# In the up product's half products, the two column pieces take turns matmul by matmul

## The chip, the cores and the metric

The kernel runs on one core of one Trainium2 chip. The metric is the device time of one launch, in microseconds. Engines are called as in the profile: PE (TensorE's matmuls), PEld (its weight loads), DVE (VectorE), ACT (ScalarE), POOL (GpSimd), SP (SyncE, which issues most transfers).

## The reference

One inference step of a one-layer trunk over 1,024 prompt tokens and 32 sample tokens: an attention mixer, then a feed-forward part with a short convolution. The part that the change touches is the first product of the feed-forward part:

```
def conv_ffn(h, conv_past, w_up, conv_w, conv_b, w_down):
    u, g = jnp.split(jnp.einsum('btd,df->btf', h, w_up), 2, axis=-1)
    u_ext = jnp.concatenate([conv_past.astype(u.dtype), u], axis=1)
    c = conv_b + u_ext[:, 0:t] * conv_w[0]
    ...
    y = jax.nn.gelu(c, approximate=True) * g
    return jnp.einsum('btf,fd->btd', y, w_down), u_ext[:, -(CONV_W - 1):]
```

All values are fp32. `h` is 1,056 x 1,024 (prompt and sample tokens together), `w_up` is 1,024 x 5,632, and `D_FF` is 2,816.

## The kernel before

**Precision.** Every fp32 operand is held as a high and a low part in a replicated fp32 type (`m_h`, `m_l` for the tokens, `ring_h`, `ring_l` or `ws_h`, `ws_l` for weights). Each product is three matmuls: high weights by high tokens, high weights by low tokens, low weights by high tokens. The helper `three` (lines 1095, 1096, 1097) issues them on one output bank. Each of these matmuls has a weight load of its own in the trace, also where two in a row use the same weights.

**The up product.** It runs over f = 0 to 21, one step for each 128 columns of u and of v. The first three steps (`plain_products`) are ordinary: 8 pieces of 24 matmuls, each piece on one bank. The other 19 (`split_products`, f = 3 to 21) use a scheme of seven half-size products in place of eight, P1, P6, P2, P7, P5, P4, P3 in this order. A half product multiplies a 512-row by 128-column weight block with 528 tokens. The 528 tokens are two column pieces of `CB` = 264, c = 0 and c = 1, each with its own PSUM bank. A piece is 4 row blocks by 3 matmuls, 12 matmuls of 264 columns. So one f is 7 x 2 x 12 = 168 matmuls and the 19 split steps hold 3,192.

**Banks.** P1 and P2 use banks 0 and 1, P6, P7 and P4 banks 2 and 3, P5 and P3 banks 4 and 5. P1, P6 and P5 start a bank afresh; P2, P7, P4 and P3 add onto what the earlier product left there. In between, the partial result has to be read out: after P1 by ACT into `p1s` (`p1_out`, line 1617 is the copy helper), after P6 and P7 by DVE into `u2s` and `u3s` (`u_sum`, line 2838), after P5, P4 and P3 by DVE into `uv` and `uext` (`out_sum`, line 2850), after P2 by ACT into `uext` (`c11_out`). Each product on a bank waits until the read before it is done. Between a product and the next that uses its banks there lies at least one whole other product.

**What else runs.** POOL forms the sums of weight blocks and the low parts (`weight_sums`, `weight_lows`), ACT the high parts (`weight_high`), each after the product that last used the slot has finished its piece 1. DVE also does the convolution (`conv_taps`, lines 2775 to 2784) and the gate (`gated`, line 2792) of f - 1, in one queue with the sums: taps 0 and 1, `u2` twice, tap 2, `u3` twice, `c22` twice, the gate, `c21` twice, `c12` twice. At f = 3 it has token preparation to do as well (`token_low`). All engines take their instructions in the written order. After f = 21 the down product begins (`step_tile`, matmuls of 512 columns, lines 1101 to 1103).

**Order inside a half product.** Piece 0 runs all of its 12 matmuls, then piece 1 all of its own:

```
for c in range(2):
    pe.wait_ge(up_act, act_evicted(f, "p1", c))
    half_product(f, "P2", c, c, m_h[:, 4:8, 0:HB], m_l[:, 4:8, 0:HB], False)
```

Of the kernel before, what the change touches and what calls it, by code (L numbers as in the profile page):

```python
# [16 lines left out]
TOK = SEQ + DEC  # L17
# [51 lines left out]
HB = TOK // 2  # L69
CB = HB // 2  # L70
# [55 lines left out]
def program(nc, x_prompt, x_sample, cache_fox_k, cache_fox_v, cache_fox_logf, cache_swa_k, cache_swa_v,  # L126
# [17 lines left out]
    def place(name, shape, dt=F32, offset=None):  # L144

        size = 4 * int(np.prod(shape[1:]))
        o = at[0] if offset is None else offset
        if offset is None:
            at[0] += (size + 31) // 32 * 32
        return nc.alloc_sbuf_tensor_at(name, shape, dt, offset=o), o  # L150
# [91 lines left out]
    m_h, _ = place("m_h", [P, KT, TOK], F32R, offset=R3)  # L242
    m_l, _ = place("m_l", [P, KT, TOK], F32R, offset=R3 + 4 * KT * TOK)
# [18 lines left out]
    tb = []  # L262
# [89 lines left out]
    bank = [nc.alloc_psum_tensor(f"bank{i}", [P, 512], F32) for i in range(8)]  # L352
# [71 lines left out]
    up_full = sem("up_full")  # L424
    up_act = sem("up_act")
    up_dve = sem("up_dve")
# [76 lines left out]
    def plain_evicted(f, kind_, t, c):  # L503
        return len(PLAIN_ORDER) * f + PLAIN_ORDER.index((kind_, t, c)) + 1

    def act_evicted(f, what, c):

        return len(PLAIN_ORDER) * PLAIN + 4 * (f - PLAIN) + dict(p1=0, c11=2)[what] + c + 1

    def dve_evicted(f, what, c):  # L510

        return 10 * (f - PLAIN) + 2 * ["u2", "u3", "c22", "c21", "c12"].index(what) + c + 1

    def blocks_made(f, name):

        return 7 * (f - PLAIN) + PRODUCTS.index(name) + 1
# [179 lines left out]
    def mix_bank(t, e):  # L696

        return bank[((7, 0), (1, 2), (3, 4))[t % 3][e]]

    def sbank(i):  # L700
        return bank[3 + i % 2]

    def merge_bank(i):

        return bank[(7, 0, 1, 2, 3, 4)[i % 6]]
# [53 lines left out]
    with nc.Block() as block:  # L759

        def flat(slot):
            return slot.rearrange("p k c -> p (k c)")
# [165 lines left out]
        def slot(name):  # L928

            i = dict(P1=0, P2=1, P6=2, P4=3, P7=4, P5=5, P3=6)[name]  # L930
            if i == 6:
                return ws_h[:, :, :], ws_l[:, :, :]
            return tuple(w[:, i // 2, 4 * (i % 2):4 * (i % 2) + 4, :] for w in (ring_h, ring_l))
# [158 lines left out]
        def _(pe):  # L1092
            def three(out, wh, wl, xh, xl, start, stop, onto=False):

                nc.tensor.matmul(out, wh, xh, start=start, stop=False, skip_group_check=onto)  # L1095
                nc.tensor.matmul(out, wh, xl, start=False, stop=False, skip_group_check=onto)  # L1096
                return nc.tensor.matmul(out, wl, xh, start=False, stop=stop, skip_group_check=onto)  # L1097

            def three_moving(out, th, tl, wh, wl, start, stop, onto=False):

                nc.tensor.matmul(out, th, wh, start=start, stop=False, skip_group_check=onto)  # L1101
                nc.tensor.matmul(out, th, wl, start=False, stop=False, skip_group_check=onto)  # L1102
                return nc.tensor.matmul(out, tl, wh, start=False, stop=stop, skip_group_check=onto)  # L1103
# [70 lines left out]
            for k in range(4):  # L1174
                mm = nc.tensor.transpose(bank[3][0:HEADS, P * k:P * k + P], cln[:, k, :], ident)
            mm.then_inc(misc_pe, 1)
            for k in range(6):
                mm = nc.tensor.transpose(bank[4][:, FT * k:FT * k + FT], cvn[:, k, :], ident[0:FT, 0:FT])
# [108 lines left out]
            for g in range(2):  # L1287
                for i, (o, w) in enumerate(((0, PAST), (PAST, DEC))):
                    s = S_SMP + 2 * g + i
                    pe.wait_ge(s_free, s - 1)  # L1290
                    for e in range(2):
                        mm = nc.tensor.matmul(sbank(s)[:, 0:w], qbd[:, 2 * g + e, :], ktc[:, 2 * g + e, o:o + w],
                                              start=(e == 0), stop=(e == 1))
# [4 lines left out]
            for g in range(2):  # L1298
# [7 lines left out]
                for e in range(2):  # L1306
                    pr = 2 * g + e
                    for k in range(5):
                        v = past[:, k, P * pr:P * pr + P] if k < 4 else fresh[0:DEC, P * pr:P * pr + P]
                        r = DEC if k == 4 else P  # L1310
                        mm = nc.tensor.matmul(bank[7][:, P * pr:P * pr + P], v, pts[0:r, k, :],
                                              start=(k == 0), stop=(k == 4))
# [88 lines left out]
            for i in range(3 * KT):  # L1401
                s, e, c = i // 6, i // 3 % 2, i % 3
                n = SLAB["ws", s]
                wh, wl = (flat(w[:, n % NSPL]).rearrange("p (k c) -> p k c", k=4)[:, :, P * e:P * e + P]
                          for w in (ring_h, ring_l))
# [7 lines left out]
                for k in range(4):  # L1413
                    mm = three(merge_bank(i)[:, 0:CH], wh[:, k, :], wl[:, k, :], ot_h[:, k, CH * c:CH * c + CH],
                               ot_l[:, k, CH * c:CH * c + CH], k == 0, k == 3)
# [10 lines left out]
            for t in range(NT + 1):  # L1426
# [4 lines left out]
                for e in range(2):  # L1431
# [3 lines left out]
                    for k in range(KT):  # L1435
# [3 lines left out]
                        elif t == 0 and (e == 0 or last):  # L1439
                            pe.wait_ge(slab_split, SLAB["wo", k] + 1)  # L1440
                        wh = wo_last_h[:, cols_e] if last else wo[k][:, 0, cols_e]
                        wl = wo_last_l[e][:, :] if last else wo[k][:, 1, cols_e]
                        mm = three_moving(mix_bank(t, e)[0:r, :], m_h[:, k, P * t:P * t + r],
                                          m_l[:, k, P * t:P * t + r], wh, wl, k == 0, last)
# [25 lines left out]
                                   k == 0, k == KT - 1)  # L1470
                    mm.then_inc(up_full, 1)

            def half_product(f, name, c, b, xh, xl, fresh_bank):

                pe.wait_ge(w_ready, blocks_made(f, name))
                wh, wl = slot(name)
                for k in range(4):
                    mm = three(bank[b][:, 0:CB], wh[:, k, :], wl[:, k, :], xh[:, k, CB * c:CB * c + CB],
                               xl[:, k, CB * c:CB * c + CB], fresh_bank and k == 0, k == 3, not fresh_bank)
                mm.then_inc(up_full, 1)  # L1480

            def split_products(f):

                first = f == PLAIN
                for c in range(2):
                    pe.wait_ge(up_act, plain_evicted(f - 1, "u", 0, c) if first else act_evicted(f - 1, "c11", c))
                    half_product(f, "P1", c, c, m_h[:, 0:4, 0:HB], m_l[:, 0:4, 0:HB], True)
                if first:
                    pe.wait_ge(t_ready[2], 1)
                for c in range(2):  # L1490
                    if first:
                        pe.wait_ge(up_act, plain_evicted(f - 1, "v", 0, c))
                    else:
                        pe.wait_ge(up_dve, dve_evicted(f - 1, "c21", c))
                    half_product(f, "P6", c, 2 + c, tb[0][0], tb[0][1], True)
                for c in range(2):
                    pe.wait_ge(up_act, act_evicted(f, "p1", c))
                    half_product(f, "P2", c, c, m_h[:, 4:8, 0:HB], m_l[:, 4:8, 0:HB], False)
                if first:
                    pe.wait_ge(t_ready[3], 1)  # L1500
                for c in range(2):
                    pe.wait_ge(up_dve, dve_evicted(f, "u2", c))
                    half_product(f, "P7", c, 2 + c, tb[1][0], tb[1][1], False)
                if first:
                    pe.wait_ge(t_ready[1], 1)
                for c in range(2):
                    if first:
                        pe.wait_ge(up_act, plain_evicted(f - 1, "u", 1, c))
                    else:
                        pe.wait_ge(up_dve, dve_evicted(f - 1, "c12", c))  # L1510
                    half_product(f, "P5", c, 4 + c, m_h[:, 0:4, HB:TOK], m_l[:, 0:4, HB:TOK], True)
                if first:
                    pe.wait_ge(t_ready[0], 1)
                for c in range(2):
                    pe.wait_ge(up_dve, dve_evicted(f, "u3", c))
                    half_product(f, "P4", c, 2 + c, tb[2][0], tb[2][1], False)
                for c in range(2):
                    pe.wait_ge(up_dve, dve_evicted(f, "c22", c))
                    half_product(f, "P3", c, 4 + c, m_h[:, 4:8, HB:TOK], m_l[:, 4:8, HB:TOK], False)

            for f in range(PLAIN):
                plain_products(f)
            for f in range(PLAIN, FT):
                split_products(f)
# [24 lines left out]
            def step_tile(name, k, t):  # L1549

                if k == 0:
                    wait_out_bank(name, t)
                ah, al, bh, bl = ops[step(name, k) % NOP]
                fresh = name in FRESH
                c = slice(P * t, P * t + P)
                return three_moving(bank[PRODUCT_BANKS[name][t]][:, :], ah[:, c], al[:, c], bh[:, :], bl[:, :],
                                    fresh and k == 0, k == HK - 1, not fresh)
# [27 lines left out]
            for name in DOWN:  # L1585
                last = name == DOWN[-1]
                for k in range(HK - GROUP if last else HK):
                    wait_operands(step(name, k))
                    if name == "P2" and k == 0:
                        pe.wait_ge(conv_done, FT)  # L1590
                        pe.wait_ge(up_dve, dve_evicted(FT - 1, "c12", 1))
                        for w in range(4):
                            mm = nc.tensor.transpose(bank[5][0:FT, P * w:P * w + P], tails[:, w, :], ident)
                        mm.then_inc(misc_pe, 1)
                    for t in range(4):
                        if t == 3 and name in SAMPLE:
                            step_sample(name, k)
                        mm = step_tile(name, k, t)
# [3 lines left out]
            for k in range(HK - GROUP, HK):  # L1602
                wait_operands(step("P3", k))
                mm = step_sample("P3", k)
            mm.then_inc(sample_full, 1)
            for t in range(4):
                for k in range(HK - GROUP, HK):
                    mm = step_tile("P3", k, t)
# [1449 lines left out]
```

## Time and profile before

| | |
|---|---|
| median of 3 runs | 1567.58 us (1566.83 to 1568.66) |
| the profiled execution's own time | 1569.79 us |
| its span, first to last instruction | 1568.0 us |
| outside the span | 1.79 us |
| PE busy | 1506.5 us, 96% |
| PEld busy | 1405.5 us, 90% |
| DVE / ACT / POOL busy | 1028.7 / 599.9 / 617.4 us |
| mean granted TensorE clock | 0.989 of full speed |

The profiled execution took 2.21 us longer than the median of the runs. Matmuls overlap each other in the trace: each is drawn 0.28 us long, but starts about 0.12 us after the one before. So the distance from start to start, called the pitch below, is what a matmul costs, not its drawn length. The timeline gives starts to 0.01 us.

### The profile page before, as it was taken

To read this page: it belongs to the slowest core of one execution; us is meant where nothing else is said; L and a number is where in the kernel's file an instruction comes from. 1 tells how busy PE (TensorE), PEld (TensorE's weight loads), DVE (VectorE), ACT (ScalarE), POOL (GpSimd) and SP (SyncE) were. 2 spreads that over 40 slices of the span, in tenths; PEclk is the share of its full clock that TensorE was granted. 3 is DMA by queue.
4 is the path that set the end of the run, shared out by engine and by line. 5 is a ranking of instruction groups with operands and counts; after the bars stand their busy time and mean duration, and the time that the engine had idled before them with its cause. 6 is when DMAs were issued, how large, how long until landed. Compare 5 with 4: busy or idle time off the path is not lost.

```text
span 1568.0 us, 25757 instructions
## 1 busy us (share of the span) xinstructions
PE 1506.5 (96%) x9819; PEld 1405.5 (90%) x9819; DVE 1028.7 (66%) x2020; ACT 599.9 (38%) x1248; POOL 617.4 (39%) x405
## 2 busy tenths in 40 slices
PE   6999999999999999999999999999999999999996
PEld 5899999999998988889787999999999999778885
DVE  6866667767674359866444796655555555578976
ACT  5133534435341235646323243233333322444463
POOL 6522232222221332225231568878787782000104
PEclk9999999999999999999999999999999999999998
DMA  6232222222122630128431112322222228723557
GB/s 197 69 87 69 73 91 65 73 69 69 30 96 74 233 105 27 52 67 287 163 114 58 44 56 83 95 73 79 80 70 70 82 83 275 243 92 114 177 189 136
DMA packets 156185, 164.87 MB, mean 105 GB/s; under 512 B 13973, under 2 KB 121881, under 8 KB 156065
## 3 DMA queue, kind: packets, MB, share of 16 engines
q1 hardware_dynamic: 119113, 108.30, 21.9%
q10 hardware_dynamic: 34840, 51.14, 9.7%
q0 software_dynamic: 2112, 3.80, 1.7%
q8 instruction: 79, 1.29, 0.3%
q14 instruction: 41, 0.34, 0.1%
HBM read 125.03 MB, written 39.85 MB: 105 GB/s over the span
## 4 chain that ended last, share of the span: by engine, by line
PE 78%; DVE 13%; ACT 2%; DMA 2%; issue 2%; POOL 2%; ACTq 1%; SPq 0%; DVEq 0%; POOLq 0%
PE bank L1095 16%; PE bank L1097 15%; PE bank L1096 15%; PE bank L1101 6%; PE bank L1103 6%; PE bank L1102 6%; PE bank L1127 4%; PE bank L1236 2%; PE bank L1207 1%; PE bank L1206 1%; DVE rowsn L2335 1%; DVE kl L2356 1%; DMA fox<-d_mfox 1%; PE bank L1575 1%; PE bank L1577 1%
## 5 line engine op out<-in xcount | busy, mean ns | idle before, releaser
L943 POOL TENSOR_TENSOR ring_h<-raw,att 128x1024 fp32r<-128x1024 f32 x48 | 101.7, 2119 | 511.4 <-PE bank L1097 501.8
L1095 PE MATMUL bank<-ht_h,ring_h 128*128 128x352 f32 x816 | 270.3, 331 | 2.0 <-POOL ring_l L944 1.6
L1097 PE MATMUL bank<-ht_h,ring_l 128*128 128x352 f32 x816 | 264.7, 324 | 0.0
L1096 PE MATMUL bank<-ht_l,ring_h 128*128 128x352 f32 x816 | 264.0, 324 | 0.0
L1095 PE MATMUL bank<-m_h,ring_h 128*128 128x264 f32 x648 | 184.2, 284 | 2.6 <-POOL ring_l L1035 1.3
L1096 PE MATMUL bank<-m_l,ring_h 128*128 128x264 f32 x648 | 184.2, 284 | 0.0
L1097 PE MATMUL bank<-m_h,ring_l 128*128 128x264 f32 x648 | 183.9, 284 | 0.0
L1095 PEld LDWEIGHTS bank<-ht_h,ring_h 128*128 128x128 f32 x816 | 155.0, 190 | 5.5 <-POOL ring_l L944 2.1
L1096 PEld LDWEIGHTS bank<-ht_l,ring_h 128*128 128x128 f32 x816 | 155.7, 191 | 0.7
L1097 PEld LDWEIGHTS bank<-ht_h,ring_l 128*128 128x128 f32 x816 | 155.1, 190 | 0.0
L944 POOL TENSOR_TENSOR ring_l<-raw,ring_h 128x1024 fp32r<-128x1024 f32 x48 | 129.8, 2704 | 3.8
L1095 PE MATMUL bank<-tb_h,ring_h 128*128 128x264 f32 x456 | 129.9, 285 | 0.0
L1097 PE MATMUL bank<-tb_h,ring_l 128*128 128x264 f32 x456 | 129.6, 284 | 0.0
L1096 PE MATMUL bank<-tb_l,ring_h 128*128 128x264 f32 x456 | 129.6, 284 | 0.0
L1095 PEld LDWEIGHTS bank<-m_h,ring_h 128*128 128x128 f32 x648 | 121.9, 188 | 3.0 <-ACT uext L1617 1.5
L1097 PEld LDWEIGHTS bank<-m_h,ring_l 128*128 128x128 f32 x648 | 122.0, 188 | 0.0
L1096 PEld LDWEIGHTS bank<-m_l,ring_h 128*128 128x128 f32 x648 | 121.7, 188 | 0.0
L1103 PE MATMUL bank<-op_bh,op_al 128*128 128x512 f32 x308 | 120.3, 391 | 0.0
L1102 PE MATMUL bank<-op_bl,op_ah 128*128 128x512 f32 x308 | 120.2, 390 | 0.0
L1101 PE MATMUL bank<-op_bh,op_ah 128*128 128x512 f32 x308 | 120.0, 389 | 0.0
L2412 DVE CUSTOM_DVE_ANT_0 ssb<-bank,negc 128x512 f32<-128x512 f32 (+2 forms) x96 | 50.9, 555 | 73.4 <-PE bank L1210 44.5
L1035 POOL TENSOR_TENSOR ring_l<-sw,ring_h 128x512 fp32r<-128x512 f32 x57 | 91.4, 1606 | 4.7 <-ACT ring_h L1617 4.7
(367 smaller groups left out, 3839.1 us busy)
## 6 DMA issues: line engine op xcount, KB each, us to landing
raw<-in_w_up SPq DMA_DIRECT2D x44, 512.0 KB, 3.8
raw<-in_w_in SPq DMA_DIRECT2D x34, 512.0 KB, 3.8
rb<-in_w_down SPq DMA_DIRECT2D x66, 256.0 KB, 2.9
d_y<-conv SPq DMA_DIRECT2D x22, 529.0 KB, 3.0
d_gate<-gst ACTq DMA_DIRECT2D x48, 176.0 KB, 1.9
a<-d_y SPq DMA_DIRECT2D x33, 256.0 KB, 5.5
ra<-d_y SPq DMA_DIRECT2D x33, 256.0 KB, 3.2
gm<-d_gate ACTq DMA_DIRECT2D x8, 528.0 KB, 4.2
```

The costliest lines, as they stand in the source:

```text
L943: order.link(nc.gpsimd.tensor_tensor(high, src, zero.to_broadcast(list(src.shape)), ALU.add))
L944: nc.gpsimd.tensor_tensor(low, src, high.bitcast(F32), ALU.subtract).then_inc(slab_split, 1)
L1035: nc.gpsimd.tensor_tensor(l, x, h.bitcast(F32), ALU.subtract).then_inc(w_ready, 1)
L1095: nc.tensor.matmul(out, wh, xh, start=start, stop=False, skip_group_check=onto)
L1096: nc.tensor.matmul(out, wh, xl, start=False, stop=False, skip_group_check=onto)
L1097: return nc.tensor.matmul(out, wl, xh, start=False, stop=stop, skip_group_check=onto)
L1101: nc.tensor.matmul(out, th, wh, start=start, stop=False, skip_group_check=onto)
L1102: nc.tensor.matmul(out, th, wl, start=False, stop=False, skip_group_check=onto)
L1103: return nc.tensor.matmul(out, tl, wh, start=False, stop=stop, skip_group_check=onto)
L1127: last = nc.tensor.transpose(o, i, ident[0:i.shape[0], 0:i.shape[0]])
L1236: nc.tensor.matmul(bank[7][:, o:SPAN], vhl[:, k, h, :], pt[:, k, o:SPAN], start=False, stop=False)
L2412: V.tensor_tensor_reduce(out=ssb[:, s % 2, o:o + w], in0=sbank(sc)[:, 0:w], in1=negc[:, h, o:o + w], scale=1.0, scalar=-3e38, op0=ALU.add, ...
```

## The change

The helper `half_product`, which did one piece, becomes `both_halves`, which does both: for every row block and each of the three terms it issues the matmul of piece 0 on bank b and then that of piece 1 on bank b + 1, with the same weights. The number of matmuls, their shapes, operands and banks, and the order of sums within each bank stay. The waits of both pieces now stand ahead of the first matmul of the product, and both pieces finish on its last two matmuls.

```
-            def half_product(f, name, c, b, xh, xl, fresh_bank):
+            def both_halves(f, name, b, xh, xl, fresh_bank):
                 pe.wait_ge(w_ready, blocks_made(f, name))
                 wh, wl = slot(name)
                 for k in range(4):
-                    mm = three(bank[b][:, 0:CB], wh[:, k, :], wl[:, k, :], xh[:, k, CB * c:CB * c + CB],
-                               xl[:, k, CB * c:CB * c + CB], fresh_bank and k == 0, k == 3, not fresh_bank)
-                mm.then_inc(up_full, 1)
+                    for i, (w, x) in enumerate(((wh, xh), (wh, xl), (wl, xh))):
+                        for c in range(2):
+                            mm = nc.tensor.matmul(bank[b + c][:, 0:CB], w[:, k, :], x[:, k, CB * c:CB * c + CB],
+                                                  start=fresh_bank and k == 0 and i == 0, stop=k == 3 and i == 2,
+                                                  skip_group_check=not fresh_bank)
+                            if k == 3 and i == 2:
+                                mm.then_inc(up_full, 1)
...
                 for c in range(2):
                     pe.wait_ge(up_act, plain_evicted(f - 1, "u", 0, c) if first else act_evicted(f - 1, "c11", c))
-                    half_product(f, "P1", c, c, m_h[:, 0:4, 0:HB], m_l[:, 0:4, 0:HB], True)
+                both_halves(f, "P1", 0, m_h[:, 0:4, 0:HB], m_l[:, 0:4, 0:HB], True)
...
-                for c in range(2):
-                    pe.wait_ge(up_act, act_evicted(f, "p1", c))
-                    half_product(f, "P2", c, c, m_h[:, 4:8, 0:HB], m_l[:, 4:8, 0:HB], False)
+                pe.wait_ge(up_act, act_evicted(f, "p1", 1))
+                both_halves(f, "P2", 0, m_h[:, 4:8, 0:HB], m_l[:, 4:8, 0:HB], False)
...
-                for c in range(2):
-                    pe.wait_ge(up_dve, dve_evicted(f, "u2", c))
-                    half_product(f, "P7", c, 2 + c, tb[1][0], tb[1][1], False)
+                pe.wait_ge(up_dve, dve_evicted(f, "u2", 1))
+                both_halves(f, "P7", 2, tb[1][0], tb[1][1], False)
```

P6, P5, P4 and P3 are changed in the same way: P6 and P5 keep the waits of both pieces, now ahead of both, and P4 and P3 wait for `u3` and `c22` of piece 1.

## Rows read from the trace of the kernel before

**Rows 1.** The page: its head, and busy time of PE, PEld and DVE.

```profile
span 1568.0 us, 25757 instructions
PE 1506.5 (96%) x9819; PEld 1405.5 (90%) x9819; DVE 1028.7 (66%) x2020; ACT 599.9 (38%) x1248; POOL 617.4 (39%) x405
```

**Rows 2.** Windows: the split stage, then the plain stage (busy us, count, clock).

```profile
965.00:1322.00 357.00, 357.00 (x2939) 357.00 (x2939) 202.80 (x336) 111.81 (x210) 274.97 (x187) 1.00 0.29 92
877.00:931.00 54.00, 54.00 (x446) 54.00 (x446) 52.13 (x26) 15.36 (x27) 32.44 (x10) 1.00 0.13 40
```

**Rows 3.** The chain that ended last, from 965 to 1322 us, by line.

```profile
by line: PE bank L1097 33.4%; PE bank L1096 33.3%; PE bank L1095 33.3%
```

**Rows 4.** Timeline of PE: ends of pieces in one round (start, drawn us, instruction).

```profile
1099.26 0.28 PE L1097 MATMUL bank<-m_h,ring_l 128*128 128x264 f32 x1
1099.38 0.28 PE L1095 MATMUL bank<-m_h,ring_h 128*128 128x264 f32 x1
...
1103.64 0.28 PE L1097 MATMUL bank<-tb_h,ring_l 128*128 128x264 f32 x1
...
1106.67 0.28 PE L1095 MATMUL bank<-tb_h,ring_h 128*128 128x264 f32 x1
```

**Rows 5.** Timeline of PE: last matmuls of pieces, plain stage, then split stage.

```profile
884.45 0.28 PE L1097 MATMUL bank<-m_h,ring_l 128*128 128x264 f32 x1
...
931.13 0.28 PE L1097 MATMUL bank<-m_h,ring_l 128*128 128x264 f32 x1
932.75 0.36 PE L1095 MATMUL bank<-m_h,ring_h 128*128 128x264 f32 x1 [1.34 <-POOL ring_l L1035]
...
965.07 0.28 PE L1097 MATMUL bank<-tb_h,ring_l 128*128 128x264 f32 x1
...
1116.76 0.28 PE L1097 MATMUL bank<-m_h,ws_l 128*128 128x264 f32 x1
...
1118.20 0.28 PE L1097 MATMUL bank<-m_h,ws_l 128*128 128x264 f32 x1
...
1119.68 0.28 PE L1097 MATMUL bank<-m_h,ring_l 128*128 128x264 f32 x1
...
1322.40 0.28 PE L1097 MATMUL bank<-m_h,ws_l 128*128 128x264 f32 x1
```

**Rows 6.** Timeline of DVE: piece 1 of two sums, then both pieces of one.

```profile
1103.96 0.43 DVE L2838 TENSOR_TENSOR u2s<-bank,p1s 128x264 f32<-128x264 f32 x1 [0.97 <-PE bank L1097]
...
1118.52 0.50 DVE L2850 TENSOR_TENSOR uext<-bank,u2s 128x232 f32<-128x232 f32 x2 [1.01 <-PE bank L1097]
...
939.01 0.77 DVE L2838 TENSOR_TENSOR u2s<-bank,p1s 128x264 f32<-128x264 f32 x2
```

**Rows 7.** Timeline of ACT: both pieces of one copy out of PSUM.

```profile
1108.62 0.65 ACT L1617 ACTIVATE uext<-bank 128x264 f32<-128x264 f32 x2
```

**Rows 8.** Timelines of DVE, then of PE, in the second split step (f = 4).

```profile
956.54 0.76 DVE L2850 TENSOR_TENSOR uv<-bank,p1s 128x264 f32<-128x264 f32 x2
...
963.13 0.77 DVE L2838 TENSOR_TENSOR u2s<-bank,p1s 128x264 f32<-128x264 f32 x2
...
963.39 0.28 PE L1097 MATMUL bank<-m_h,ring_l 128*128 128x264 f32 x1
963.62 0.39 PE L1095 MATMUL bank<-tb_h,ring_h 128*128 128x264 f32 x1
```

**Rows 9.** A window at the lower clock; timelines of PE there and later.

```profile
81.00:87.00 6.00, 6.00 (x24) 0.50 0.54 123
...
82.47 0.49 PE L1097 MATMUL bank<-ht_h,ring_l 128*128 128x352 f32 x1
82.76 0.49 PE L1095 MATMUL bank<-ht_h,ring_h 128*128 128x352 f32 x1
...
630.22 0.32 PE L1097 MATMUL bank<-ht_h,ring_l 128*128 128x352 f32 x1
630.38 0.32 PE L1095 MATMUL bank<-ht_h,ring_h 128*128 128x352 f32 x1
```

More of the change, by code:

```diff
@@ L1494, in split_products @@
                         pe.wait_ge(up_dve, dve_evicted(f - 1, "c21", c))
-                    half_product(f, "P6", c, 2 + c, tb[0][0], tb[0][1], True)
-                for c in range(2):
-                    pe.wait_ge(up_act, act_evicted(f, "p1", c))
-                    half_product(f, "P2", c, c, m_h[:, 4:8, 0:HB], m_l[:, 4:8, 0:HB], False)
+                both_halves(f, "P6", 2, tb[0][0], tb[0][1], True)
+                pe.wait_ge(up_act, act_evicted(f, "p1", 1))
+                both_halves(f, "P2", 0, m_h[:, 4:8, 0:HB], m_l[:, 4:8, 0:HB], False)
                 if first:
                     pe.wait_ge(t_ready[3], 1)
-                for c in range(2):
-                    pe.wait_ge(up_dve, dve_evicted(f, "u2", c))
-                    half_product(f, "P7", c, 2 + c, tb[1][0], tb[1][1], False)
+                pe.wait_ge(up_dve, dve_evicted(f, "u2", 1))
+                both_halves(f, "P7", 2, tb[1][0], tb[1][1], False)
                 if first:
@@ L1510, in split_products @@
                         pe.wait_ge(up_dve, dve_evicted(f - 1, "c12", c))
-                    half_product(f, "P5", c, 4 + c, m_h[:, 0:4, HB:TOK], m_l[:, 0:4, HB:TOK], True)
+                both_halves(f, "P5", 4, m_h[:, 0:4, HB:TOK], m_l[:, 0:4, HB:TOK], True)
                 if first:
                     pe.wait_ge(t_ready[0], 1)
[L1514 to L1519, printed above, removed]
+                pe.wait_ge(up_dve, dve_evicted(f, "u3", 1))
+                both_halves(f, "P4", 2, tb[2][0], tb[2][1], False)
+                pe.wait_ge(up_dve, dve_evicted(f, "c22", 1))
+                both_halves(f, "P3", 4, m_h[:, 4:8, HB:TOK], m_l[:, 4:8, HB:TOK], False)
             for f in range(PLAIN):
```

## The prediction

> **What bounds the kernel now.** I read the page first. PE is busy for 96% of the span, DVE for 66% [rows 1], so the question is whether the change makes PE's stream shorter or puts holes into it. The windows come next. From 965 to 1322 us, where 17 of the 19 split steps and most of another run, PE is busy in all 357 us and the granted clock is 1.00, the 2.4 GHz level [rows 2]. The chain of waits over the same stretch holds nothing but the three lines of the matmul helper, a third each [rows 3]: PE waits for nobody there. What sets the stage is the pitch times the number of matmuls.
>
> The pitch comes from counted matmuls between two starts. From 965.07 us (the last matmul of piece 0 of P7 at f = 4) to 1322.40 us (the last one of f = 21) there are 7 pieces of f = 4 and 17 steps of 168, so 84 + 2,856 = 2,940 matmuls in 357.33 us: 121.54 ns each [rows 5]. All 3,192 of the split steps at that pitch are 388.0 us, 25% of the time. One nanosecond of pitch is worth 3.19 us, which is 0.20% of the time, and 0.2% (3.1 us) is about what a measurement of this kernel can tell from no change.
>
> **The change, part by part.**
>
> *The same matmuls in another order.* Nothing is added or removed: 3,192 matmuls with 3,192 loads stay. What moves is the bank: before, PE goes to another bank after 12 matmuls, after the change it does so at every one. A run of one matmul per bank is not in the trace, so I bound its cost by how the pitch reacts to changes of bank that are there.
>
> First the single step. Piece 0 of P1 ends at 1099.26 us and piece 1 begins in the other bank at 1099.38, a pitch of 0.12 us [rows 4], like that within a piece. If writing onto the same bank again were what costs the pitch its excess, the matmul behind a change of bank would start earlier, and it does not, to the 0.01 us that the view gives.
>
> Then the mean. In the plain stage a bank takes 24 matmuls in a row, in the split stage 12. From 884.45 to 931.13 us lie the 16 pieces of 24 of f = 1 and 2, 384 matmuls in 46.68 us, 121.56 ns each [rows 5]. Twice as many changes of bank per matmul leave the pitch where it was, 121.54 against 121.56. The rounding of the starts makes that 0.02 +- 0.03 ns in favour of more changes. The step from 24 to 12 adds one change per 24 matmuls, the change under study adds 22 per 24 more. Stretched by 22, the difference is -0.5 +- 0.7 ns, so -1.5 us with ends at -3.6 and +0.6 us. I do not take that mean as the value, because the two stages read other tiles and the reading order matters too.
>
> How much it matters is seen in the pieces. Twelve matmuls of the last piece of P3 take 1.44 us (1116.76 to 1118.20), the twelve of the next P1 take 1.48 us (1118.20 to 1119.68) [rows 5], 120 against 123 ns, with the same shapes and no wait. So an order of operand addresses can be worth a nanosecond or two in a single piece. Over all fourteen pieces of a step these differences average out at 121.5. After the change the addresses stay and only their order is new. I take 0 as the value. For the ends I take half of the difference between these pieces and the mean, 0.75 ns below and above, so -2.4 and +2.4 us. The lower end by the stretched difference, -3.6 us, reaches further and takes its place.
>
> *Same weights twice as often.* Before, one matmul in three has the weights of the matmul before it (the first two of a triple); after, four in six. Each keeps its own load; now there is one for every matmul [rows 1]. In a triple the starts are 0.12 us apart whether the weights are new or not, so I cost this at nothing, within the ends above.
>
> *The waits of both pieces come first.* In a steady step this is hidden. P6 ends with a matmul at 1103.64 us, DVE begins the sum of piece 1 at 1103.96, 0.32 us later, and is done 0.43 us after that [rows 4, 6]. After the change both pieces are full at that same moment. Two sums in a row take 0.77 us [rows 6], so the second is read at 0.32 + 0.77 = 1.09 us behind the last matmul's start. P7, which needs both, begins at 1106.67 us, 3.03 us behind it [rows 4]. The cover left is 1.9 us. It is P2, a whole product of 24 x 121.5 = 2.92 us. The same holds for P7 to P4, P5 to P3 and P4 to the next P6, each with one or more products between. The read of piece 1 after P3 comes in two instructions, together 0.50 us in place of 0.43 [rows 6], which makes the pair 0.77 + 0.07 = 0.84 us, still far below. ACT's copies of both pieces take 0.65 us [rows 7].
>
> What queues behind the later reads: on DVE, taps 0 and 1 of the convolution follow the two `c12` sums. Before, piece 0 was read during piece 1's matmuls; now both wait for the end, so the taps start 0.34 us later (0.84 - 0.50). DVE idled 0.97 us before the last `u2` sum and 1.01 us before the last `c12` sum [rows 6], so it catches up before the next product needs it. On ACT the weight copies behind `p1_out` start 0.3 us later. They feed weights of the step after, a step of 20.4 us away, and POOL's work is released by the piece 1 that ends when it did. No transfer is issued by an engine that becomes later by more than this.
>
> *Start of the split stage.* DVE is behind there, since it prepares tokens. At f = 4 it begins the two `u2` sums at 963.13 us and is done at 963.90 [rows 8]. P7's first matmul starts at 963.62 us, 0.23 us behind the one before in place of 0.12, since it waits for the first sum only (963.13 + 0.43 = 963.56, and 0.06 us for the signal). After the change it waits for both: 963.90 + 0.06 = 963.96 us. That is +0.34 us, once. The `c21` sums of f = 3 are both done by 956.54 + 0.76 = 957.30 us [rows 8], before P6 of f = 4 needs them: P2 ends at 963.39 + 0.12 = 963.51, two products less is 957.67. That cover is 0.37 us. At f = 5 and later nothing of this is left, as the chain shows [rows 3]. The last step hands over to the down product with DVE's queue 0.3 us later, which lies behind a whole down step that does not need it.
>
> *The sum.* Pitch 0, steady waits 0, start +0.34 us, end 0: the profiled execution's 1569.79 us becomes 1570.13. It stood 2.21 us above the median of the runs, so the median to expect is 1567.9 us.
>
> **The rivals.**
>
> *Coming back to the same bank is what costs (faster).* At 2.4 GHz and a column per cycle 264 columns are 110.0 ns; the pitch is 121.5 [rows 2, 5]. Matmuls of 352 columns follow each other at 160 ns (630.22 to 630.38) [rows 9], 38.5 ns for 88 more columns, 0.44 ns each, so about 115 of the 121.5 goes with the columns. If the rest, 6 to 11.5 ns, were a wait for the last write to the same bank, alternating would save 19 to 37 us and give 1531 to 1549 us. Against it stands the step between banks at 0.12 us. A weaker form, 1 to 3 ns, is what the pieces' differences allow: 1558 to 1564.5 us. The Trainium skill (TensorE: Matmul & The Clock Gate, "Back-to-back issue gap") gives a bare gap of 112.5 ns for this width, and says that in a stream of loads and matmuls both set the spacing; by the bare gap the sum would be 28.8 us lower, but it names no cost of a bank, and the trace shows 121.5.
>
> *The new order is a bad one (slower).* Each matmul reads 1,056 bytes further on in the same row and then back; if the pieces' slow pattern (123 ns) became the rule, 1.5 ns x 3,192 = 4.8 us, 1567.9 + 4.8 = 1572.7 us. It decides from 1 ns on.
>
> *The reads are no longer covered (slower).* If a product had to wait for the second read in every step, as at f = 4, it would cost 0.34 us x 19 = 6.5 us for each such product, 1574 us. It decides when DVE reaches the pair 1.9 us or more late. The idle time of 1 us ahead of its sums speaks against it.
>
> *The clock falls (slower).* A stretch at granted clock 0.50, the 1.2 GHz level, is in the trace from 81 to 87 us; matmuls of 352 columns follow each other there at 0.29 us against 0.16 [rows 9]. Six such microseconds cost 6 x (1 - 0.16 / 0.29) = 2.7 us. In the split stage it is 1.00 throughout, and the one new hole is 0.34 us, shorter than the 1.62 us from 931.13 to 932.75 us that are there now, between the two windows at 1.00 [rows 2, 5]. The Trainium skill (TensorE: Matmul & The Clock Gate, "A second HAM failure mode: psum-queue depth-cycling") speaks against such a change: a kernel that cycled through banks idled briefly and often, and its clock went up and down. Here the pairs leave no gap for that, and this rival gets 1 in 100.
>
> **How the numbers follow.** The forecast, a time within 0.2% of before: 0.72. Faster through the bank: 0.14. Slower through the order: 0.10, through uncovered reads: 0.03, through the clock: 0.01. So faster 0.14, same 0.72, slower 0.14. The likeliest case alone spans 1567.9 - 3.6 = 1564.3 to 1567.9 + 2.4 = 1570.3. The range is drawn a little wider to take in the near parts of the two pitch rivals: 1564.0 to 1571.2 us.
>
> **What the profile after would show.** The pitch over the counted 2,940 matmuls between 121 and 122 ns, the clock at 1.00, the chain in that stretch still only matmul lines, DVE's `u2` sums as pairs of 0.77 us begun 0.3 us behind P6, and P7 at f = 4 starting 0.34 us later. The prediction is wrong if the pitch moves by more than 1 ns, which the view of starts shows at once, or if the view of waits names DVE or ACT ahead of a product after f = 4.

## The result and the profile after

The changed kernel takes 1570.76 us (median of 12 runs, 1567.8 to 1575.71) against 1567.53 us (12 runs, 1564.53 to 1570.48) for the kernel before. The ratio is 1.0023, with a 95% interval from 1.0013 to 1.0032: 3.2 us slower (2.0 to 5.0 us by the interval), a small loss, but the interval lies above 1. The time is inside the range of the prediction, 0.4 us below its upper end, but the likeliest case there (a time within 0.2% of before) put its upper end at 1570.3 us. The rival "the new order is a bad one", at 1572.7 us, is nearer than the forecast of 1567.9 us.

The page of the changed kernel says almost nothing. Its span is 0.4 us longer than that before [rows 1]:

```profile
span 1568.4 us, 25626 instructions
PE 1505.3 (96%) x9819; PEld 1405.0 (90%) x9819; DVE 1031.9 (66%) x2020; ACT 598.1 (38%) x1248; POOL 619.5 (39%) x405
```

The window of the split stage in the changed kernel shows more. Its columns are those of [rows 2]:

```profile
930.30:1323.30 393.00, 391.58 (x3191) 391.18 (x3192) 231.31 (x362) 122.15 (x235) 305.70 (x204) 1.00 0.29 92
```

The stage began 2.4 us earlier here than in [rows 5], by differences in stages that the change does not touch, and this hides most of the loss in the span of this one execution. So the stage has to be compared alone. PE's timeline after the change gives the first matmul of the split stage, the first of f = 5, and the first of the down product:

```profile
930.37 0.48 PE L1480 MATMUL bank<-m_h,ring_h 128*128 128x264 f32 x2 [1.34 <-POOL ring_l L1035]
...
973.35 0.41 PE L1480 MATMUL bank<-m_h,ring_h 128*128 128x264 f32 x2
...
1323.43 0.39 PE L1101 MATMUL bank<-op_bh,op_ah 128*128 128x512 f32 x1
```

The stage takes 1323.43 - 930.37 = 393.06 us. Before it took 389.77 us, from 932.75 to 1322.52, one pitch behind the last row of [rows 5]. That is +3.29 us, and the medians differ by 3.23 us. The 17 steps from f = 5 on hold 2,856 matmuls in 350.08 us: 20.593 us for a step and 122.58 ns for a matmul. In the kernel before, the same two starts are

```profile
975.38 0.28 PE L1095 MATMUL bank<-m_h,ring_h 128*128 128x264 f32 x1
...
1322.52 0.39 PE L1101 MATMUL bank<-op_bh,op_ah 128*128 128x512 f32 x1
```

so 347.14 us, 20.420 us for a step and 121.55 ns for a matmul. The pitch has grown by 1.03 ns.

Nothing waits there. The chain of the changed kernel from 965 to 1322 us is the one matmul line, as in [rows 3]:

```profile
by line: PE bank L1480 100.0%
964.98 357.03 PE bank L1480 x2913
```

The reads of the banks went as forecast. DVE's timeline in one step after the change, then PE's around it (P6's last matmuls and P7's first):

```profile
1102.95 0.77 DVE L2838 TENSOR_TENSOR u2s<-bank,p1s 128x264 f32<-128x264 f32 x2 [1.92 <-PE bank L1480]
```

```profile
1102.57 0.41 PE L1480 MATMUL bank<-tb_h,ring_l 128*128 128x264 f32 x2
1102.81 0.41 PE L1480 MATMUL bank<-m_h,ring_h 128*128 128x264 f32 x2
...
1105.76 0.40 PE L1480 MATMUL bank<-tb_h,ring_h 128*128 128x264 f32 x2
```

The last matmul of P6 is the second of the pair at 1102.57, so at about 1102.69. The pair of sums begins 0.26 us behind it, lasts 0.77 us and ends at 1103.72, 2.04 us before P7 begins. DVE had been idle for 1.92 us before it. At f = 4 the new wait shows:

```profile
960.73 0.77 DVE L2838 TENSOR_TENSOR u2s<-bank,p1s 128x264 f32<-128x264 f32 x2
```

```profile
960.97 0.41 PE L1480 MATMUL bank<-m_h,ring_l 128*128 128x264 f32 x2
961.55 0.51 PE L1480 MATMUL bank<-tb_h,ring_h 128*128 128x264 f32 x2 [0.17 <-DVE u2s L2838]
```

P7 starts at 961.55, 0.05 us after the pair of sums ends at 961.50. Its distance from the matmul before (961.10) is 0.45 us; it was 0.23 us in [rows 8].

### The profile page after: what moved, and what is told of

It reads as the page before. It is cut to its first block, busy times and chain, and to the rows that moved or that the text cites. A ratio compares the mean times of both kernels' runs of the same rounds, so it can differ in the third digit from the quotient of the medians.

```text
span 1568.4 us, 25626 instructions
## 1 busy us (share of the span) xinstructions
PE 1505.3 (96%) x9819; PEld 1405.0 (90%) x9819; DVE 1031.9 (66%) x2020; ACT 598.1 (38%) x1248; POOL 619.5 (39%) x405
## 4 chain that ended last, share of the span: by engine, by line
PE 76%; DVE 13%; POOL 3%; DMA 2%; ACT 2%; issue 2%; ACTq 1%; SPq 0%; DVEq 0%; POOLq 0%
PE bank L1480 23%; PE bank L1095 8%; PE bank L1097 7%; PE bank L1096 7%; PE bank L1101 6%; PE bank L1103 6%; PE bank L1102 6%; PE bank L1127 4%; PE bank L1236 2%; PE bank L1207 1%; PE bank L1206 1%; DVE rowsn L2335 1%; DMA fox<-d_mfox 1%; POOL ring_l L1035 1%; DVE kl L2356 1%
## 5 line engine op out<-in xcount | busy, mean ns | idle before, releaser
L1035 POOL TENSOR_TENSOR ring_l<-sw,ring_h 128x512 fp32r<-128x512 f32 x57 | 94.6, 1664 | 4.8 <-ACT ring_h L1617 4.7
L1480 PE MATMUL bank<-m_h,ring_h 128*128 128x264 f32 x456 | 92.9, 285 | 2.5 <-POOL ring_l L1035 1.3
L1480 PE MATMUL bank<-m_h,ring_l 128*128 128x264 f32 x456 | 93.5, 287 | 0.0
L1480 PE MATMUL bank<-tb_h,ring_l 128*128 128x264 f32 x456 | 93.2, 286 | 0.0
L1480 PE MATMUL bank<-tb_h,ring_h 128*128 128x264 f32 x456 | 92.8, 285 | 0.2 <-DVE u2s L2838 0.2
L1480 PE MATMUL bank<-m_l,ring_h 128*128 128x264 f32 x456 | 92.9, 285 | 0.0
L1480 PE MATMUL bank<-tb_l,ring_h 128*128 128x264 f32 x456 | 92.7, 285 | 0.0
L1617 ACT ACTIVATE pt_h<-bank 128x512 fp32r<-128x512 f32 (+2 forms) x96 | 43.6, 488 | 122.9 <-PE bank L1237 86.3
L1617 ACT ACTIVATE ring_h<-sw 128x512 fp32r<-128x512 f32 x57 | 35.6, 632 | 142.7 <-POOL sw L1028 122.9
L1786 ACT ACTIVATE ssb<-ssb,att 128x128 f32<-128x128 f32 (+3 forms) x64 | 49.7, 777 | 82.7 <-DVE att L2419 82.6
```

The lines of the kernel that those rows point to most:

```text
L1035: nc.gpsimd.tensor_tensor(l, x, h.bitcast(F32), ALU.subtract).then_inc(w_ready, 1)
L1480: mm = nc.tensor.matmul(bank[b + c][:, 0:CB], w[:, k, :], x[:, k, CB * c:CB * c + CB], start=fresh_bank and k == 0 and i == 0, stop=k == 3 ...
L1617: return nc.scalar.activation(out, in_, cp, scale=scale)
```

## The experiments

The question was which part of the change costs a nanosecond per matmul. All kernels are made from the changed one. They replace the loops of `both_halves` by this body, in which weights, tokens and banks each have a sequence of their own. In the cuts below, what stands behind a `#` is a note for the reader.

```
+                after = [(k, i, c) for k in range(4) for i in range(3) for c in range(2)]
+                before = [(k, i, c) for c in range(2) for k in range(4) for i in range(3)]
+                weights, moving, banks = ...
+                place_of = [c for _, _, c in banks]
+                for j in range(24):
+                    (kw, iw, _), (kx, ix, cx), c = weights[j], moving[j], place_of[j]
...
+                    mm = nc.tensor.matmul(bank[b + c][:, 0:CB], terms[iw][0][:, kw, :],
+                                          terms[ix][1][:, kx, CB * cx:CB * cx + CB], ...)
```

The figure to compare is the steady step: the start of f = 5 to the start of the down product, divided by 17. Within a trace the 17 steps agree to 1 ns, with one exception of 12 ns in all traces, and kernels that read the tokens in the same order have the same step in traces taken on different chips, so one profile of each is enough to tell 0.01 us. The distance between P2's last matmul and P7's first at f = 4 is given as "the hole".

**Only the waits.**

```
+                weights, moving, banks = before, before, before
```

> The waits of both pieces stand ahead of the product, as in the changed kernel, but piece 0 then runs its 12 matmuls and piece 1 its own, as before. The loss of the change is 0.17 us in each steady round of 168 matmuls (20.59 against 20.42 us) and about 0.3 us once at f = 4. Theory A, the order of matmuls is what costs: the steady round is 20.42 us here, the step at f = 4 stays late by about 0.3 us, in all 0.3 us over the kernel before. Theory B, the waits in front cost something in every round: the round is 20.59 us here too, and the time is 3 us over the kernel before.

```profile
974.91 0.28 PE L1485 MATMUL bank<-m_h,ring_h 128*128 128x264 f32 x1
...
1322.05 0.39 PE L1101 MATMUL bank<-op_bh,op_ah 128*128 128x512 f32 x1
```

347.14 / 17 = 20.420 us, the step of the kernel before. The hole is 0.51 us; it was 0.23 us before and is 0.45 us in the changed kernel. The time is 1567.98 us (10 runs) against 1566.92 (13 runs), a ratio of 1.0 (0.9989 to 1.0011), which rules out the 3 us of theory B as well. Theory A holds: the waits in front cost a few tenths once, the order of the matmuls costs the rest.

**Only the banks, and only the reads.**

```
+                weights, moving, banks = before, before, after    # banks only
+                weights, moving, banks = after, after, before     # reads only
```

> The 24 matmuls of a product read weights and tokens in the order of the kernel before, and write the banks b, b + 1, b, b + 1 in turn. What is summed in a bank is thus not the product of its own piece; the amount of work, the waits and all shapes stay. Theory A1, the change of bank at each matmul costs 1 ns: the steady round is 20.59 us. Theory A2, the order in which operands are read costs: the round is 20.42 us.

> The counterpart: weights and tokens are read in the order of the changed kernel, and the first 12 matmuls write bank b, the next 12 bank b + 1. What is summed in a bank is not the product of its own piece; the amount of work, the waits and all shapes stay. Theory A1, change of bank: the steady round is 20.42 us. Theory A2, order of the reads: 20.59 us. If both share in it, the two runs add up to 20.59 - 20.42 = 0.17 us over the round before.

PE's timeline with the banks in turn:

```profile
970.50 0.28 PE L1485 MATMUL bank<-m_h,ring_h 128*128 128x264 f32 x1
...
1317.64 0.39 PE L1101 MATMUL bank<-op_bh,op_ah 128*128 128x512 f32 x1
```

and with the reads in the new order:

```profile
971.55 0.41 PE L1485 MATMUL bank<-m_h,ring_h 128*128 128x264 f32 x2
...
1321.63 0.39 PE L1101 MATMUL bank<-op_bh,op_ah 128*128 128x512 f32 x1
```

Banks in turn: 347.14 / 17 = 20.420 us. Reads in the new order: 350.08 / 17 = 20.593 us. In this stream a change of bank at every matmul costs nothing and gains nothing; the whole loss of the steady step follows the order in which operands are read.

**Triples in turn.** Three matmuls of piece 0, three of piece 1, on their own banks:

```
+                triple = [(k, i, c) for k in range(4) for c in range(2) for i in range(3)]
+                weights, moving, banks = triple, triple, triple
```

> The pieces take turns after each row block: three matmuls of piece 0, three of piece 1, on their banks, so the bank changes every third matmul and weights repeat as before. Theory A1, each change of bank costs: 8 changes in 24 in place of 24 (2 in the kernel before), so (8 - 2) / (24 - 2) of 0.17 us is 0.05 us, the round is 20.47 us. Theory A2 with the token pieces in turn as the costly part: about the same 20.47 us. Theory A2 with the repeated weights as the costly part: 20.42 us.

```profile
975.01 0.28 PE L1486 MATMUL bank<-m_h,ring_h 128*128 128x264 f32 x1
...
1321.02 0.40 PE L1101 MATMUL bank<-op_bh,op_ah 128*128 128x512 f32 x1
```

346.01 / 17 = 20.353 us, 121.15 ns for a matmul. No theory expected this: the step is shorter than before, by 0.067 us. So taking turns is not bad in itself.

**Weights apart from tokens.**

```
+                weights, moving, banks = after, before, before    # weights
+                weights, moving, banks = before, after, before    # tokens
```

> Only the sequence of weight tiles is that of the changed kernel (four of six matmuls use the weights of the one before them); token pieces and banks go in the order of the kernel before. What is summed is thus not the product; the amount of work and all shapes stay. Theory W, the order of weights costs: the steady round is 20.59 us. Theory M, the token pieces in turn cost: 20.42 us. Theory I, what counts is how the two sequences meet: neither this run nor its counterpart need be at one of the two values, and they need not add up to the 0.17 us.

> The counterpart: only the sequence of token tiles is that of the changed kernel, weights and banks go in the order before. What is summed is not the product; the amount of work and all shapes stay. Theory W: the steady round is 20.42 us. Theory M: 20.59 us. Theory I: a third value.

PE's timeline with the new sequence of weights alone:

```profile
971.97 0.28 PE L1485 MATMUL bank<-m_h,ring_h 128*128 128x264 f32 x1
...
1319.11 0.39 PE L1101 MATMUL bank<-op_bh,op_ah 128*128 128x512 f32 x1
```

and with the new sequence of tokens alone:

```profile
974.67 0.41 PE L1485 MATMUL bank<-m_h,ring_h 128*128 128x264 f32 x2
...
1324.76 0.39 PE L1101 MATMUL bank<-op_bh,op_ah 128*128 128x512 f32 x1
```

New sequence of weights: 347.14 / 17 = 20.420 us. New sequence of tokens: 350.09 / 17 = 20.593 us. Theory M holds. Of the three sequences that the change alters, only that of the token reads (the moving operand) moves the pitch; whether one matmul in three or four in six repeat their weights makes no difference.

**Another distance between the pieces.** Piece 1 starts 1,024 bytes behind piece 0 in place of 1,056:

```
-                                          ... CB * cx:CB * cx + CB
+                                          ... 256 * cx:256 * cx + CB
```

> The changed kernel's order, but piece 1 reads its 264 columns from 1,024 bytes behind piece 0 in place of 1,056 (columns 256 to 519 in place of 264 to 527), so that both start at the same place of a 64-byte line. Eight columns are computed twice and eight not at all. Theory L, the jump between two different places of a line costs the nanosecond: the steady round falls to about 20.42 us. If it stays near 20.59 us, the place of the start is not the cause.

> The order of the kernel before with the same 1,024 bytes between the pieces; eight columns are computed twice and eight not at all. Theory L in its narrow form (only the jump costs): the steady round stays at 20.42 us, as there is one jump in 12 matmuls. If a start in the middle of a line costs by itself, it falls below 20.42 us here too.

PE's timeline in the new order, then in the order before:

```profile
971.63 0.40 PE L1485 MATMUL bank<-m_h,ring_h 128*128 128x264 f32 x2
...
1322.05 0.39 PE L1101 MATMUL bank<-op_bh,op_ah 128*128 128x512 f32 x1
```

```profile
976.50 0.28 PE L1485 MATMUL bank<-m_h,ring_h 128*128 128x264 f32 x1
...
1322.85 0.39 PE L1101 MATMUL bank<-op_bh,op_ah 128*128 128x512 f32 x1
```

The new order takes 20.613 us with it (20.593 without), the order before 20.373 us (20.420). Both moved, and neither as theory L says in its narrow form. Its wide form, that a start in the middle of a line costs by itself, fits the order before, which became shorter, but not the new order, which became longer. The 64-byte line is only the unit of this theory; no run here shows that there is one. What the two runs show is that 32 bytes in a starting address are enough to change the pitch.

**Is it the neighbour?** In the run with triples, the mean pitch one matmul behind a step from one piece to the columns right behind them was 123.2 ns, and 120.5 to 121.1 ns elsewhere. This was thin ground: in the first three row blocks of a product that mean is 121.3 to 121.8 ns, and only the fourth, at 128.0 ns, lifts it. Three more runs test this, all with the right operands: pairs and triples in which piece 1 is two row blocks away, and the old order with the terms rearranged so that the same tokens are read twice running.

```
+                far = [((k + 2 * c) % 4, i, c) for k in range(4) for i in range(3) for c in range(2)]   # pairs
+                far = [((k + 2 * c) % 4, i, c) for k in range(4) for c in range(2) for i in range(3)]   # triples
+                same = [(k, i, c) for c in range(2) for k in range(4) for i in (0, 2, 1)]               # same tile
```

> The pieces take turns matmul by matmul as in the changed kernel, with the right operands, but piece 1 is two row blocks away from piece 0 (row blocks 2, 3, 0, 1 in place of 0, 1, 2, 3). So no matmul reads the token columns that lie right behind those of the matmul before it. Theory N, a matmul whose tokens are the neighbour in the same row of the ones just read costs about 2.5 ns (read from the run with triples, where the pitch behind such a pair is 123.2 against 120.7 ns): half of the matmuls lose it, the steady round falls from 20.59 to about 20.4 us. Theory T, taking turns between the pieces costs as such: 20.59 us.

> Piece 0 and then piece 1 as before, but the three terms come as high weights by high tokens, low weights by high tokens, high weights by low tokens, so the same token columns are read twice in a row in one of three matmuls. Theory N in its wide form (reading the same row of the same tile again): 56 of 168 transitions cost 2.5 ns more, the steady round rises from 20.42 to 20.56 us. Theory N in its narrow form (only the columns right behind): 20.42 us. Theory T: 20.42 us.

> The pieces take turns by triples as in the run with triples (20.35 us a round), but piece 1 is two row blocks away. Theory N: the neighbour transitions, 28 in a round, lose 2.5 ns each, the round falls to 20.28 us. Theory T: it stays at 20.35 us.

Far pairs: 20.493 us, between 20.42 and 20.59. Far triples: 20.407 us, more than the 20.353 of the near ones where theory N wanted less. Neither is the value of theory T, 20.59 and 20.35 us. The same tile twice:

```profile
973.49 0.28 PE L1486 MATMUL bank<-m_h,ring_h 128*128 128x264 f32 x1
...
1320.63 0.39 PE L1101 MATMUL bank<-op_bh,op_ah 128*128 128x512 f32 x1
```

347.14 / 17 = 20.420 us, and each of the 168 pitches of a step is that of the run with only the waits changed. Theories N and T fall. The last result says something else: to read the high tile where the low one was read changes nothing. The two lie 33,792 bytes apart in `m_h` and `m_l` and 8,448 in the `tb` tiles, and both are multiples of 256.

**The remainder by 256.** That led to the last theory, R: of a starting address only the remainder by 256 bytes counts. It has a sharp test: move piece 1 by 256 bytes, and all should stay.

```
-                                          ... CB * cx:CB * cx + CB
+                                          ... 200 * cx:200 * cx + CB
```

> The changed kernel's order, but piece 1 reads its 264 columns from 800 bytes behind piece 0, which is 1,056 less 256 (columns 200 to 463 in place of 264 to 527): 64 columns are computed twice and 64 not at all. The two pieces are no longer neighbours. Theory R, the pitch follows the starting address of the tokens only through its remainder by 256 bytes: the steady round is again 20.59 us and the pitches go through the same sequence, matmul by matmul. Theory N, or any that needs the real distance or the neighbourhood: another round and another sequence, as 1,024 bytes gave (20.61 us, other pitches) and two row blocks gave (20.49 us).

PE's timeline of the shifted run, from f = 5 on:

```profile
972.27 0.41 PE L1485 MATMUL bank<-m_h,ring_h 128*128 128x264 f32 x2
...
1322.36 0.39 PE L1101 MATMUL bank<-op_bh,op_ah 128*128 128x512 f32 x1
```

350.09 / 17 = 20.593 us. The pitches of P1 in a steady step, read from the starts in the traces (ns, means over 14 steps; the 1,024-byte run beside them):

```
changed kernel  122 122 117 121 122 128 124 126 119 123 125 126 122 119 122 125 122 129 121 125 121 124 125 126
shifted by 256  123 122 117 121 123 128 124 126 119 123 125 126 122 119 122 125 122 129 121 125 121 124 125 126
1,024 bytes     120 120 123 122 122 124 122 124 122 124 123 124 122 122 126 127 116 122 122 124 122 124 123 124
```

The first two agree in every matmul of the step to 0.15 ns on average over the steps (the 1 ns seen here is rounding). Theory R holds in this test.

The far triples are a second test of it, which was not planned as one. Moving piece 1 by two row blocks is 8,448 bytes in `m_h` and `m_l`, a multiple of 256, but 4,224 bytes in the `tb` tiles, which leaves a remainder of 128. In the traces P1, which reads `m_h` and `m_l`, has the pitches of the near triples to 0.1 ns in all 24 matmuls; P2, P5 and P3, which read the same two tiles but come behind a product on `tb`, have them too, P2 from the seventh matmul on, P5 and P3 from the third. P6, P7 and P4, which read `tb`, have other pitches, by up to 7.5 ns. So in the triples 8,448 bytes change nothing and 4,224 do.

The steady steps by the sequence of the token reads, in us. The runs in which only waits, banks, weights or the order of the three terms were changed stand with the kernel before, those with the new reads or the new tokens alone with the changed kernel:

| sequence | near, 1,056 bytes | other |
|---|---|---|
| piece by piece (before) | 20.420 | 20.373 at 1,024 bytes |
| triples in turn | 20.353 | 20.407 two row blocks away |
| matmul by matmul (changed) | 20.593 | 20.613 at 1,024 bytes, 20.593 at 800, 20.493 two row blocks away |

## Why the prediction held in its range and missed in its likeliest case

**The outcome.** The prediction gave itself a sign of being wrong, a pitch that moves by more than 1 ns, and the sign came: 121.55 to 122.58 ns, outside the 121 to 122 ns that the profile after was to show. The forecast, a time within 0.2% of before, was missed too, by a little: the ratio is 0.23% above 1, with an interval from 0.13% to 0.32%. That the time still fell inside the range is in part luck. The range had been widened beyond the likeliest case to take in the near part of this rival, and the interval of the ratio, 1569.6 to 1572.5 us, reaches beyond its end at 1571.2 us.

**What bounds the kernel.** Right: the split stage is pitch times count. (The window from 965 us holds half of the step at f = 4, 84 of 168 matmuls, not most of it; the count of 2,940 is right.) Its growth of 3.29 us agrees with the difference of the medians, 3.23 us.

**The bank.** Right, and now shown: with only the banks in turn the step stays at 20.420 us. The argument from bank changes that are in the trace was sound for the bank. It could not speak for the reads, which change in the same edit. Only the lower end of the likeliest case, -3.6 us, came from it; the upper end, +2.4 us, came from the next term.

**The order of the operand addresses.** This is the term that was mis-sized: "I take 0 as the value", with ends at -2.4 and +2.4 us. It measured 0.173 us a step, 1.0 ns a matmul, 17 steps x 0.173 = 2.95 us in the steady part. The first two steps, f = 3 and 4, grew by another 0.35 us (42.63 to 42.98 us), 0.22 of them in the hole at f = 4. The prediction had seen a sign of this term in [rows 5], pieces of 120 and 123 ns with the same shape, and then assumed that such differences would average out in the new order too. They do average within a sequence, but each sequence has a mean of its own: 121.15, 121.55 and 122.58 ns for the three that keep their pieces side by side. The rival "the new order is a bad one" had the kind of mechanism and the point from which it decides (1 ns), with a chance of only 0.10. Its picture, reading 1,056 bytes further on and then back, is not the cause as such: with 800 bytes the step is the same. The scatter of the pieces could not tell ahead whether the new order would be faster or slower, and half of it, 0.75 ns, was too narrow an end.

**Same weights twice as often.** Right at nothing: the new sequence of weights alone leaves the step at 20.420 us.

**The waits in a steady step.** Right: the pair of sums lasts 0.77 us, and 2.0 us of cover are left where 1.9 were forecast.

**The start at f = 4.** Right in kind. P7's distance grew from 0.23 us to 0.45, so +0.22 in place of +0.34 us. In the twelve other kernels, which all wait for both pieces, the hole was 0.41 to 0.68 us, so +0.18 to +0.44. As each kernel was profiled once, it stays open how much of this differs between kernels and how much between executions.

**The clock.** It stayed at 1.00 through the stage, although PE changes bank 23 times within a product where it had changed once. So nothing is seen here of the clock going up and down that the Trainium skill (TensorE: Matmul & The Clock Gate, "A second HAM failure mode: psum-queue depth-cycling") reports.

**The other rivals.** A faster pitch through the bank is refuted by the run with only the banks changed. Uncovered reads are refuted by the chain above, which holds nothing but matmuls, and by the run with only the waits changed.

## What stays open

Why the starting address of the moving operand matters is not settled. What is shown is that the sequences of weights and banks have no part in it, that 256 bytes less between the pieces change nothing in the new order and 8,448 more nothing in the triples, and that 32 bytes do change the pitch. Theory R is not the whole account. In the far pairs, P3 reads its tokens with the same remainders as in the changed kernel, matmul by matmul, and still has other pitches (its first six are 120 120 122 120 120 126 against 122 121 120 126 121 125 ns). Its last pitches differ as well (119 123 122 118 against 126 121 122 119 ns). P2 of the far pairs, in contrast, has the pitches of the changed kernel from its fifteenth matmul on. So more than 24 matmuls of history can count, or something beside the remainder does. Nor is "the same pitches" finer than 0.7 ns between any two traces: the kernel before and the run with only the waits changed have the same step of 20.420 us and differ by up to that in single matmuls. Which sequence would be the best one was not tried.

The triples in turn shorten the stage to 388.89 us (932.12 to 1321.02 us in its trace), 0.88 us less than the kernel before with the wait at f = 4 counted, which is 0.06% and below what a measurement tells. The one execution took 1567.66 us. It is no proven gain.

## What to carry to other kernels

An edit that only reorders matmuls can still have a price, or a gain, in a stream where PE is the bound. Here it was a matter of which addresses follow each other on the moving operand; with 3,000 matmuls a nanosecond decides. Measure the pitch between two counted starts in the profile. Here a step repeats to the nanosecond where the time of a launch scatters by 6 to 8 us, so one profile tells more of this stage than twelve runs. And when an edit changes two things at once (banks and reads), evidence on one of them is no evidence on the sum.

## What the hardware showed that was not expected

The pitch of 264-column matmuls is no constant, but a fixed sequence which repeats in every step: between 116 and 127 ns in the kernel before, 116 and 129 ns in the changed one, and up to 133 ns in the triples. It depends on the starting addresses of the moving operand: the step is the same under a change of bank at every matmul, under the other sequence of weights, or with 256 bytes less between the pieces, and different under 32 bytes. The mean over a step runs from 121.15 to 122.70 ns with the matmuls' number and shape unchanged.
